# Scale and bias of the gating branch's layer norm: GpSimd with rows in SBUF in place of VectorE with rows in PSUM banks

## The reference

```
def layer_norm(x, g, b, eps=LN_EPS):
    xf = x.astype(jnp.float32)
    mu = jnp.mean(xf, axis=-1, keepdims=True)
    xc = xf - mu
    y = xc * lax.rsqrt(jnp.mean(xc * xc, axis=-1, keepdims=True) + eps)
    return (y * g.astype(jnp.float32) + b.astype(jnp.float32)).astype(x.dtype)

def sgu_branch(uv, ln_g, ln_b, w_s, b_s):
    uv = jax.nn.gelu(uv, approximate=False)
    u, v = jnp.split(uv, 2, axis=-1)
    v = layer_norm(v, ln_g, ln_b)
    v = v.reshape(bsz, nc, SGU_CHUNK, SGU_GROUPS, SGU_GROUP_DIM)
    w = w_s * jnp.tril(jnp.ones((SGU_CHUNK, SGU_CHUNK), w_s.dtype))
    mixed = jnp.einsum('gts,bcsgd->bctgd', w, v) + jnp.swapaxes(b_s, 0, 1)[None, None, :, :, None]
    return u * mixed.reshape(bsz, s, SGU_WIDTH)
```

## Time and profile before

| | |
|---|---|
| median of three runs | 1888.12 us |
| the profiled execution's own time | 1885.84 us |
| its span, first to last instruction | 1883.8 us |
| mean granted TensorE clock | 0.999 |
| TensorE busy | 1858.0 us (99%) |
| VectorE busy | 1502.6 us (80%) |
| ScalarE busy | 1269.2 us (67%) |
| GpSimd busy | 29.5 us (2%) |

### The profile page before, as it was taken

One profiled execution on the slowest core, in us unless ns is written; L12 is line 12 of the kernel. 1 busy time (PEld: TensorE's weight loads), 2 busy tenths in 40 slices (PEclk: granted clock), 3 DMA queues, 4 the chain that ended last, 5 costly groups with the idle time before them and its releaser, 6 DMA issues.

```text
span 1883.8 us, 23545 instructions
## 1 busy us (share of the span) xinstructions
PE 1858.0 (99%) x9155; PEld 1548.7 (82%) x9155; DVE 1502.6 (80%) x1887; ACT 1269.2 (67%) x1616; POOL 29.5 (2%) x28
## 2 busy tenths in 40 slices
PE   7999999999999999999999999999999999999998
PEld 6778888888889687888888888888888888888787
DVE  6877675654568767676799999989999899998987
ACT  5766575454446765754677877778777787787775
POOL 0000000000000000000000000000000000000000
PEclk9999999999999999999999999999999999999999
DMA  7445425555464545237999999999999999999992
GB/s 256 134 156 179 135 84 185 179 179 179 167 206 160 179 135 179 90 135 262 348 373 374 368 381 376 391 376 378 382 368 393 379 378 383 360 394 384 378 390 82
DMA packets 223650, 509.32 MB, mean 270 GB/s; under 512 B 9046, under 2 KB 15540, under 8 KB 223284
## 3 DMA queue, kind: packets, MB, share of 16 engines
q1 hardware_dynamic: 218694, 495.15, 72.3%
q0 software_dynamic: 3120, 11.54, 2.2%
q10 hardware_dynamic: 1726, 1.14, 0.2%
HBM read 500.47 MB, written 7.34 MB: 270 GB/s over the span
## 4 chain that ended last, share of the span: by engine, by line
PE 76%; DVE 2%; ACT 1%; issue 0%; DMA 0%; POOLq 0%; DVEq 0%; PEldq 0%
PE ps L1124 13%; PE ps L1126 13%; PE ps L1125 13%; PE ps L1117 6%; PE ps L1115 6%; PE ps L1116 6%; PE ps L1202 4%; PE ps L1204 3%; PE ps L1203 3%; PE ps L1030 2%; PE ps L1005 1%; DVE w_lo L2080 1%; PE ps L1444 1%; PE ps L1329 1%; PE ps L1455 1%; PE ps L1281 1%
## 5 line engine op out<-in xcount | busy, mean ns | idle before, releaser
L2080 DVE TENSOR_TENSOR w_lo<-piece,w_hi 128x1024 fp32r<-128x1024 f32 (+1 forms) x742 | 854.8, 1212 | 79.0 <-ACT w_hi L1646 76.4
L1646 ACT ACTIVATE w_hi<-piece 128x1024 fp32r<-128x1024 f32 (+1 forms) x742 | 731.2, 1048 | 68.9 <-PE ps L1117 37.8
L1124 PE MATMUL ps<-w_hi,xg_hi 128*128 128x512 f32 x896 | 354.6, 396 | 1.3 <-POOLq L951 1.1
L1126 PE MATMUL ps<-w_hi,xg_lo 128*128 128x512 f32 x896 | 349.2, 390 | 0.0
L1125 PE MATMUL ps<-w_lo,xg_hi 128*128 128x512 f32 x896 | 348.7, 389 | 0.0
L2179 DVE TENSOR_TENSOR w_lo<-piece,mixer_hi 128x1024 fp32r<-128x1024 f32 x184 | 220.7, 1221 | 93.5 <-ACT mixer_hi L1703 93.0
L1703 ACT ACTIVATE mixer_hi<-piece 128x1024 fp32r<-128x1024 f32 x184 | 191.1, 1057 | 126.5 <-PE ps L1204 105.7
L1126 PEld LDWEIGHTS ps<-w_hi,xg_lo 128*128 128x128 f32 x896 | 168.2, 188 | 35.9
L1115 PE MATMUL ps<-w_hi,hid_hi 128*128 128x512 f32 x504 | 197.6, 392 | 0.0
L1124 PEld LDWEIGHTS ps<-w_hi,xg_hi 128*128 128x128 f32 x896 | 168.3, 188 | 35.5 <-issue 1.9
L1117 PE MATMUL ps<-w_hi,hid_lo 128*128 128x512 f32 x504 | 196.4, 390 | 0.0
(11 more groups left out here) (368 smaller groups left out, 2451.7 us busy)
## 6 DMA issues: line engine op xcount, KB each, us to landing
piece<-in_moe_w_gate SPq DMA_DIRECT2D x56, 2048.0 KB, 10.4
piece<-in_moe_w_up SPq DMA_DIRECT2D x56, 2048.0 KB, 10.4
piece<-in_moe_w_down SPq DMA_DIRECT2D x56, 2048.0 KB, 9.8
piece<-in_w_in SPq DMA_DIRECT2D x30, 2048.0 KB, 9.3
piece<-in_ffn_w_gate SPq DMA_DIRECT2D x5, 2048.0 KB, 7.9
piece<-in_ffn_w_up SPq DMA_DIRECT2D x5, 2048.0 KB, 7.8
piece<-in_ffn_w_down SPq DMA_DIRECT2D x5, 2048.0 KB, 7.8
piece<-in_w_br_ssd SPq DMA_DIRECT2D x4, 2048.0 KB, 7.9
```

What stands on the lines that cost most here:

```text
L1124: pe.matmul(b, a_hi, hi[:, cs_], start=(kk == 0), stop=False)
L1126: last = pe.matmul(b, a_lo, hi[:, cs_], start=False, stop=(kk == KD - 1))
L1646: act.activation(hi, slots[s][:, at_:at_ + n], ACT.Copy).then_inc(S["hi_made"], 1)
L2080: dve.tensor_tensor(w_lo[s][:, at_:at_ + n], slots[s][:, at_:at_ + n], hi.bitcast(F32), ALU.subtract).then_inc(S["lo_made"], 1)
```

## The change

`ln_g` and `ln_b` are no longer in the table `vec`. Two transfers on GpSimd's queue broadcast them as rows to all partitions, into `ln_rows`, 128 x 2 x 1024. That buffer lies over `prev` and `xd`, and under `merged`; so the transfers wait until VectorE has read `xd` for the last time (`xd_used`), and VectorE waits for `v_normed` before it first writes `merged`. GpSimd multiplies and adds on whole tiles of 128 x 1024. The four banks `lng0` to `lnb1` and their 16 matmuls are gone; the banks of all other jobs are the same as before. `vec_used`, which lets the next layer's vectors be loaded, is signalled earlier.

```
-    j += ["wt0", "wt1", "lng0", "lng1", "lnb0", "lnb1"]
+    j += ["wt0", "wt1"]
...
+        ln_rows, _ = piece(at, 2, D)
         merged, at = piece(at, NT, D)
...
-            for L in range(1, DEPTH):
-                pool.wait_ge(x_made, 4 * L)
-                pool.memset(xin[:, :, :, 0:TAPS - 1], 0.0).then_inc(zeros_made, 1)
+            for L in range(DEPTH):
+                layer[id(pool)] = L
+                if L:
+                    pool.wait_ge(x_made, 4 * L)
+                    pool.memset(xin[:, :, :, 0:TAPS - 1], 0.0).then_inc(zeros_made, 1)
+                passed(pool, "xd_used", 1)
+                for i, src in enumerate(("sgu_ln_g", "sgu_ln_b")):
+                    pool.dma_start(ln_rows[:, i, :], A[src][L:L + 1, :].to_broadcast([P, D])).then_inc(ln_in, 16)
+                pool.wait_ge(ln_in, 32 * L + 32)
+                for t in range(NT):
+                    passed(pool, "v_scale_made", t + 1)
+                    pool.tensor_tensor(vs[:, t, :], vs[:, t, :], ln_rows[:, 0, :], ALU.mult).then_inc(S["v_gained"], 1)
+                for t in range(NT):
+                    passed(pool, "v_gained", t + 1)
+                    pool.tensor_tensor(vs[:, t, :], vs[:, t, :], ln_rows[:, 1, :], ALU.add).then_inc(S["v_normed"], 1)
...
-                pe.wait_ge(vec_in, L * 192 + 192)
+                pe.wait_ge(vec_in, L * 160 + 160)
...
-                for what, row in (("lng", "ln_g"), ("lnb", "ln_b")):
-                    for hh in range(2):
-                        b = bank(f"{what}{hh}")
-                        for i in range(4):
-                            r = ROWS[row] + 4 * hh + i
-                            last = pe.matmul(b[:, i * P:(i + 1) * P], ident[:, r:r + 1].to_broadcast([P, P]), vec[:, :],
-                                             start=True, stop=True)
-                        done(last)
...
-            load_vectors(act, 0, slice(0, 8))
+            load_vectors(act, 0, slice(0, 6))
...
+                passed(dve, "xd_used", 1)
                 given(dve, "cb")
...
                 for t in range(NT):
-                    mark(dve.tensor_scalar(vs[:, t, :], vs[:, t, :], mv[:, t, 0:1], lrs[:, t:t + 1],
-                                           ALU.subtract, ALU.mult))
-                sync()
-                for what, op in (("lng", ALU.mult), ("lnb", ALU.add)):
-                    rest_mixer(NEEDED["gate_ssd01"])
-                    for hh in range(2):
-                        b = take(dve, f"{what}{hh}")
-                        for t in range(NT):
-                            if what == "lnb":
-                                given(dve, f"lng{hh}")
-                            cut = vs[:, t, hh * N:(hh + 1) * N]
-                            ins = dve.tensor_tensor(cut, b, cut, op)
...
-                dve.tensor_copy(small[:, 510:511], mv[:, 0, 0:1]).then_inc(S["v_normed"], 2)
+                    dve.tensor_scalar(vs[:, t, :], vs[:, t, :], mv[:, t, 0:1], lrs[:, t:t + 1], ALU.subtract, ALU.mult
+                                      ).then_inc(S["v_scale_made"], 1)
+                rest_mixer(NEEDED["gate_ssd01"])
...
                 turn_keys()
+                passed(dve, "v_normed", 2)
                 merge("ssd", 0)
```

More of the change, by code:

```diff
@@ L44 @@
 for _name, _n in (("mix", 8), ("ffn", 8), ("conv_b", 12), ("conv_w", 48), ("ssd", 8), ("q", 2), ("kv", 1),
-                  ("sgu_b", 8), ("ln_g", 8), ("ln_b", 8), ("q_head", 1), ("k_head", 1)):
+                  ("sgu_b", 8), ("q_head", 1), ("k_head", 1)):
     ROWS[_name] = _at
@@ L130, in place_banks @@
         elif JOB[name] < JOB["kT00"]:
-            bank[name] = (JOB[name] + 2) % 8
+            bank[name] = (JOB[name] + (2 if JOB[name] <= JOB["wt1"] else 6)) % 8
         elif name.startswith("kT"):
@@ L330 @@
     "latmean_made": 1, "latroot_made": 1, "lat_normed": 2, "kv_copied": 8, "gated": 12, "hsq_made": 4, "hmean_made": 1,
-    "hroot_made": 1, "hnorm_made": 3, "max_made": 12, "prob_made": 12, "o_made": 12, "var_made": 1, "vroot_made": 1,
+    "hroot_made": 1, "hnorm_made": 3, "max_made": 12, "prob_made": 12, "o_made": 12, "var_made": 1, "vroot_made": 1, "v_scale_made": 2, "v_gained": 2, "xd_used": 1,
     "v_normed": 2, "fsquared": 2, "fmean_made": 1, "frooted": 1, "frs_made": 1, "h_hi_made": 4, "h_lo_made": 4,
@@ L589, in hybrid_trunk @@
         vec_used = sem("vec_used")
+        ln_in = sem("ln_in")
         x_made = sem("x_made")
@@ L619, in hybrid_trunk @@
             "kv_copied", "gated", "hsq_made", "hmean_made", "hroot_made", "hnorm_made", "max_made",
-            "prob_made", "o_made", "var_made", "vroot_made", "v_normed", "fsquared", "fmean_made",
+            "prob_made", "o_made", "var_made", "vroot_made", "v_scale_made", "v_gained", "xd_used", "v_normed", "fsquared", "fmean_made",
             "frooted", "frs_made", "fn_made", "sg_made", "h_made", "t_full", "hid_hi_made", "hid_made",
@@ L775, in hybrid_trunk @@
             ("mix", "mix_norm_g", 8), ("ffn", "ffn_norm_g", 8), ("conv_b", "conv_b", 12), ("ssd", "ssd_norm_g", 8),
-            ("q", "q_norm_g", 2), ("kv", "kv_norm_g", 1), ("ln_g", "sgu_ln_g", 8), ("ln_b", "sgu_ln_b", 8))]
+            ("q", "q_norm_g", 2), ("kv", "kv_norm_g", 1))]
         def load_vectors(eng, L, some):
@@ L840, in _ @@
                 if L:
-                    load_vectors(sp, L, slice(0, 8))
+                    load_vectors(sp, L, slice(0, 6))
                 load_head_vectors(sp, L)
@@ L1246, in merged_split @@
                         given(pe, f"mT{t}{hh}")
+                pe.wait_ge(bank_full, L * len(JOBS) + JOB["vec"] + 1)
+                pe.sem_inc(vec_used, 1)
                 s, _, width = panel("lat")
@@ L1377, in _ @@
                     turn_over(f"wt{i}", [sgu_raw[:, g, :] for g in range(4 * i, 4 * i + 4)])
-                for what, row in (("lng", "ln_g"), ("lnb", "ln_b")):
-                    for hh in range(2):
-                        b = bank(f"{what}{hh}")
-                        for i in range(4):
-                            r = ROWS[row] + 4 * hh + i
-                            last = pe.matmul(b[:, i * P:(i + 1) * P], ident[:, r:r + 1].to_broadcast([P, P]), vec[:, :],
-                                             start=True, stop=True)
-                        done(last)
-                vec_read = turn[0]
                 for i in BOTH_GATES_FIRST:
                     close_part("ssd", i, xh, lambda t: passed(pe, "y_normed", t + 1))
-                    if i == 0:
-                        pe.wait_ge(bank_full, L * len(JOBS) + vec_read)
-                        pe.sem_inc(vec_used, 1)
                 def turn_heads(w_no, name, src):
@@ L2374, in _ @@
                     cut = xh[:, 1, g * N:(g + 1) * N]
-                    mark(dve.tensor_tensor(cut, cut, xd[:, g * N:(g + 1) * N], ALU.add))
+                    ins = dve.tensor_tensor(cut, cut, xd[:, g * N:(g + 1) * N], ALU.add)
+                    if g == 0:
+                        mark(ins)
+                    else:
+                        ins.then_inc(S["xd_used"], 1)
+                passed(dve, "xd_used", 1)
                 given(dve, "cb")
```

7 lines of the change are left out of this document (removed).

## The result

The changed kernel takes 1895.79 us (median of 6 runs, 1894.53 to 1897.03) against 1887.55 for the kernel before on the same chip: the ratio is 1.0046, with a 95% interval of 1.0035 to 1.0056. It is 8.2 us slower, where 4.5 us faster had been predicted; the time lies outside the range. The profiled execution took 1897.03 us, its span 1895.2.

The account below looks back on a forecast made before the run. TensorE is busy 99%, but ScalarE and VectorE carry the chain for 30 us before br_ssd0. Two layers at 2.0 us plus 0.5 at the start gave 4.5 us, from 1888.12 to 1883.6; range 1881.0 to 1893.5.

Parts of the forecast that it names:

- Part 1: TensorE before the gate panel: 16 matmuls less, 3.5 us, of which 1.2 come through after a 2.3 us stall.
- Part 2: VectorE before br_ssd0: eight instructions and a copy less, moving all behind them forward by 5.08 us.
- No collision: Rival: GpSimd costs VectorE nothing; 2.9 us a layer gained, 1881.8 us in all; chance 0.20.
- Part 5: Kernel start: two vector transfers fewer let everything up to 15.15 us move earlier by 0.5, bounds 0 and 0.65.
- Part 3: Four GpSimd operations a layer, 2.3 us each, their own time hidden; br_ssd0 2.4 us early, gain 2.0 a layer.
- d: What GpSimd costs VectorE before br_ssd0: taken as 2.7 us, between nothing and 7.3; up to 2.2 costs nothing.
- I take the middle: one more collides in full: GpSimd's first operation costs VectorE 0.4 us, one more 2.3, one runs beside bank reads, the last waits for v_normed.
- Full lock, in turns: Rival: VectorE's pieces and GpSimd's operations alternate, holding VectorE 7.3 us a layer; 3.9 us slower, 1892.0; chance 0.30.
- The two places in the prediction that give 1895: Full lock, in turns with 2.7 us operations; and a rival with GpSimd late at 7 us each, chance 0.05.
- The clock behind the stall: Rival: TensorE's new stall at the gate panel's fourth quarter costs more, as by lower clock; about 1887; chance 0.05.
- Part 4: Two 512 KB transfers a layer, at about 112 us in layer 0: 0 to 3.3 us late, covered, cost 0.

Follow-up runs that it names:

- e7: Changed kernel with GpSimd's four operations a layer on one column instead of 1024, and all buffers at the old addresses: 1880.59 us, ratio 0.9965.
- e5: Changed kernel with cols padded by 16 columns, so that every buffer behind it lies at the address of the kernel before: 1889.86 us, ratio 1.0017.
- e1: Changed kernel with GpSimd's four operations a layer on one column instead of 1024, waits and transfers kept: 1885.65 us, ratio 0.9991.
- e6: Kernel before with the arena alone 64 bytes higher: 1892.14 us, ratio 1.0028.
- e2: Kernel before with four GpSimd operations of 128x1024 on a scratch buffer added in each layer: 1892.10 us, ratio 1.0023.
- e9: Kernel before with 64 bytes of padding ahead of everything, so that x, hT and the arena move together: 1887.43 us, ratio 1.0000.
- e10: Kernel before with the arena alone 128 bytes higher: 1893.03 us, ratio 1.0026.
- e15: Kernel before with hT_hi and the buffers behind it up to the keys 64 bytes higher: 1894.60 us, ratio 1.0040.
- e17: Kernel before with the arena alone 32 bytes higher: 1893.03 us, ratio 1.0031.
- e8: Changed kernel at old addresses, GpSimd's operations halved to 512 columns and started after the keys are scaled, ScalarE waiting instead of VectorE: 1880.61 us, ratio 0.9966.
- e13: Changed kernel with hT_hi and the convolution and query buffers behind it moved 64 bytes higher: 1899.71 us, ratio 1.0067.
- e12: Changed kernel at the old addresses, each GpSimd operation cut into two of 512 columns: 1884.81 us, ratio 0.9986.

## Why the prediction was wrong, point by point

**Part 1 held.** The stall before the gate panel's fourth quarter was put at 2.3 us, 2.7 with a first collision of 0.4, and is 2.26 (2.28 in layer 0), with VectorE's `w_lo` as its end. At the old addresses it is 2.09 without GpSimd's work (e7) and 2.38 with it (e5); both are 0.2 to 0.3 us less than worked out.

**Part 2 held.** Without GpSimd's work and at the old addresses (e7) the two layers gain 3.0 and 1.4 us, where *No collision* had 2.9 a layer; layer 1's smaller gain is the lower clock behind a stall (eight matmuls, 1.6 us). The medians stand 6.7 us apart, where that rival had 6.3, but that near hit is partly luck: the stretches gave 4.4 of the 5.8 us, and the start gave more than the 0.5 taken (Part 5).

**Part 3 failed: the value of d.** The length of GpSimd's operation was taken right: 2.3 us, 2.2 measured from the turns. What failed is "I take the middle: one more collides in full". The first costs 0.4 us as taken, and all three others collide in full. The VectorE pieces give d = 11.43 (719.40 to 730.83) less 4.6 = 6.8 us; *Full lock, in turns* had said 7.3, the forecast 2.7. At the old addresses that is a stretch of 32.8 and 32.5 us (e5), where the rival had 32.2 (30.0 and its 2.2), and 1889.86 us, 2.6 us slower than before, where it had 3.9. So this step alone turns the sign: with every address kept the change still loses. The argument against it was that VectorE's instructions follow each other without a gap; that says nothing on who comes next when another engine is waiting. The rule that I had cited from the Trainium skill (SBUF — State Buffer, "Who interferes with whom") is that two such instructions contend and the first to start has the shared ports for its whole length; the trace agrees, with 3.34 us from start to start. I had cited it and then taken a value that contradicts it. The two places in the prediction that give 1895, nearest to what was measured, match by chance: an operation takes 2.2 us and not 2.7, and GpSimd was never late.

**Part 3 named the wrong place for the new wait.** It feared for the wait at `v_normed`. That wait never held: GpSimd ends at 729.8. The late piece was the second panel's fourth quarter, 736.38 to 737.52 in the chain above, because VectorE reaches it only after `yT_lo`. The kernel before has the same order, and no slack there: TensorE's timeline of before, at that fourth quarter, shows a wait already.

```profile
728.42 0.39 PE L1204 MATMUL ps<-mixer_hi,hT_lo 128*128 128x512 f32 x1
729.17 0.50 PE L1202 MATMUL ps<-mixer_hi,hT_hi 128*128 128x512 f32 x1 [0.36 <-DVE w_lo L2179]
```

I had counted only three quarters of that panel.

**The clock behind the stall was priced in a rival, not in the sum.** In the changed kernel 12 matmuls in layer 1 and 8 behind each of the two stalls in layer 0 run at the lower level, 28 x 0.20 = 5.6 us; before had none in these stretches. It isn't an addend of the measured sum, since it sits inside the shares above.

**Nothing in the prediction covered the address.** The step that failed is unwritten: that a smaller table changes nothing outside the stretch. Of the 8.2 us 5.1 to 5.9 come from there (e1 to e7, e5), and e6 shows 4.9 on the kernel before. The diff showed it: `N_ROWS` sizes `cols`, and the arena is allocated behind it.

**Part 4 held.** The transfers are issued at 112.77 us in layer 0 and nothing waits for them.

**Part 5: the way was right, the size is not settled.** The first TensorE instruction moved from 10.65 to 10.19, 0.46 us against the 0.5 taken:

```profile
10.19 0.45 PE L1167 MATMUL ps<-const,vec 128*128 128x128 f32 x1 [10.19 <-DMA vec<-in_kv_norm_g]
```

That match is luck. In the eight traces with twelve vectors (before, e2, e6, e9, e10, e15 to e17) this instruction starts at 10.50 to 11.89 us, in the eleven with ten at 8.89 to 10.39; the medians are 1.6 us apart, beyond the upper bound of 0.65. Nor does the 0.46 reach the rest of the kernel in the profiled pair: the full clock is granted from 18.19 us on before and from 19.41 on after, and the first product of the mixer starts at 27.76 and at 28.07. Over all traces that product starts at 27.76 to 30.06 us with twelve vectors and at 26.40 to 28.07 with ten, 1.7 us apart in the median. No run changes the vectors alone.

## What to carry to other kernels

An engine at 2% of the span isn't free: before work goes to GpSimd, look at what VectorE does in that stretch, and if it reads two operands from SBUF there, count every GpSimd operation in full, cut them short, or start them where VectorE is ahead. Before a buffer's size is changed, look at what is allocated behind it, and keep the distances (here 256 bytes more were harmless, the only multiple tried); a change that is spread evenly over stages that it does not touch is the sign of it. A removed wait on a bound engine is worth only what the next producer allows, and an idle stretch of two microseconds on TensorE can cost most of as much again in clock (1.4 to 1.6 us behind 2.1 in e7 and e8, and nothing in their layer 0).

## What the runs showed of the hardware that was not expected

- TensorE's pace on 128x512 products hangs on how its operand buffers lie to each other: 227.2 to 227.5 ns with the layout before, with all of it shifted, or with the arena shifted by 256 bytes; 231 to 233 ns with the arena, or one of its buffers, shifted by 32, 64 or 128. Over a dense round it repeats to 0.02 us. Only products that read an operand moved against their others are slow; those that read `ssd_hi`, `yT_hi`, `hid` or, in the expert part, `xg` stay at about 227 in the changed kernel. There the step from a product with `hT_lo` to one with `hT_hi` carries most of it (227.6 ns before, 235.0 after, in the 50 us from 100 us on; the two other steps 227.0 and 227.4 before, 228.9 and 229.3 after), while in e13 the three steps are alike (233.2 to 233.7). Why it is so stays open. That e15 slows the products with `ssd_hi` and leaves those with `yT_hi` alone points at TensorE's own reads; no run shows what in them takes longer.
- GpSimd and VectorE alternate strictly, one instruction each, when both read two operands from SBUF: 3.34 us a pair at 1024 columns, 2.23 with GpSimd at 512 (e12). VectorE instructions with one operand in a bank run beside it unheld (4.86 us for eight, against 4.87).
- The lower clock level does not follow every stall: e8 has a stall of 2.09 us in layer 1 with seven slow matmuls behind it, and about the same stall in layer 0 with none. What decides between them stays open.
